# Second norm of a decoder layer in two column halves, two up units opened together, and the group differences spread over the products

## Chip, cores and metric

One core of one Trainium2 chip runs the kernel. The metric is the device time of one execution in microseconds (us), the median of several runs.

## What is computed

One decoder layer over 2048 prompt tokens and 8 x 4 sample tokens, D = 1024, DFF = 2816, all in float32:

```python
h = rms_norm(x, norm1_g) * (1 + scale1) + shift1
...
x = x + gate1 * (jnp.concatenate([o_sb, o_mlp], axis=-1) @ w_out)
h2 = rms_norm(x, norm2_g) * (1 + scale2) + shift2
up = h2 @ w_up
conv = conv_b + sum(conv_w[i] * buf[:, i:i + t] for i in range(CONV_W))
g_ff, v_ff = jnp.split(conv, 2, axis=-1)
x = x + gate2 * ((jax.nn.silu(g_ff) * v_ff) @ w_down)
```

The convolution is causal and three wide; `buf` is `up` with its two predecessor rows in front (the halo). The sample tokens also attend over 8192 cached positions that are read page by page.

## The kernel before

The kernel has four stages; the change lies in the last, `finish_layer`. It holds its activations transposed: 128 features on the partitions, tokens along the free axis. The prompt is worked in four chunks of 512 tokens (c = 0 to 3); the 32 sample tokens ride with chunk 3, so that its tiles are 544 wide.

A chunk is a list of 38 **units** (`unit_order`): 4 out units (w_out), 22 up units (one 128-column pair of gate and value each), and 12 down units in three groups of four (depths 8, 8 and 6 tiles of `hidden`), slipped in between the up units as soon as their part of `hidden` exists. A unit is a 2 x 2 block product done in **seven products** (a Strassen-Winograd scheme) instead of eight: products 1, 2, 6, 5, 7, 3, 4 in that order, each of four matmuls 128x128 by 128x256 (three in the last down group; a matmul leaves two records). Four weight sums (`weight_sums`, GpSimd, L1675 to L1680) belong to each unit, and four **differences** of the moving operand (`difference`, VectorE, L1531) to each group of units that share it: one set for the out units, one for the up units, three for the down groups. Product 6 of a group's first unit needs two of the four, product 7 three, product 4 all.

`product_order` writes the order of the 266 products of a chunk: product 1 of a unit, then product 4 of the unit before, then 2, 6, 5, 7, 3; only the last out unit and the last unit close with their own product 4 straight behind 3. `multiply` (L1368) issues them. Four PSUM banks serve two units in turn; a product that reuses a bank waits until its last result is drained: in up units by ScalarE for products 1, 6, 5, 4 (`collect`, L1461) and by VectorE for 2, 7, 3 (`combine`, L1591); in out and down units by VectorE for all seven (`add_gated`, L1555, which adds into x).

`chunk_plan` interleaves the rest with the products, and every engine walks the same list in order. A product costs 1.75, the steps of the norm are given costs too (3.5, 4, 4, 4, 12, 2: 42.5 in all), and the pieces of the sample attention (SCORE, WEIGH, MOVE, SUM for each of 64 steps, in chunks 0 to 2) are spread evenly over the summed cost. Of a step, SCORE (L962), MOVE (L968) and SUM (L976) are TensorE's, WEIGH (L1051, L1038, L1042) and the copy after MOVE (L1046) VectorE's, the two gates after SCORE (L1011, L1012) ScalarE's. The pages are issued by SyncE in order: K pages of step N when SCORE of N-1 is done, V pages of N when SUM of N-1 is done (L922, L925). Behind the last pages of a chunk SyncE issues the next chunk's input `act_in` (`load_in`, L1300).

**The norm** stands between the last out unit and up unit 0. ScalarE squares x (L1418, L1419), TensorE sums over the partitions with a matrix of ones (L1381; L1383 for the sample columns), ScalarE takes the root (`root`, L1423), VectorE the reciprocal (`invert`, L1627), VectorE and GpSimd multiply four tiles each (`scale`, L1632 and L1694), ScalarE applies gain and shift (`modulate`, L1434), VectorE makes the four up differences. All of it is 512 columns wide.

**The differences** of the down groups stand four in a row behind product 3 of up units 10 and 18; those of the next chunk's out units four in a row behind product 5 of down unit 2 of the last group (chunks 0 and 1) or product 2 of down unit 3 (chunk 2). `first_taps` (VectorE) copies the halo into `raw` (L1605) and the new halo out (L1611), then does two taps of the convolution (L1620; L1622 for the samples); `last_tap` (ScalarE, L1439) does the third ahead of it.

```python
follow = {(AT_UNIT[UP, 10, 0], 3): [("diff", d0, i) for i in range(4)],
          (AT_UNIT[UP, 18, 0], 3): [("diff", d1, i) for i in range(4)],
...
ahead = (AT_UNIT[DOWN, 2, 2], 5) if c < NCH - 2 else (AT_UNIT[DOWN, 3, 2], 2)
```

## Time and profile before

| | us |
|---|---|
| median of 3 runs (3638.83 to 3641.12) | 3639.74 |
| the profiled execution, its own time | 3645.24 |
| span in its profile, first to last instruction | 3643.5 |
| of the span, the last stage from its first product | 1296.9 to 3643.5 |
| chunks 0, 1, 2, 3 of it, each from where the chunk before hands over | 611, 599, 591, 546 |

TensorE's busy time counts a matmul from its start to its modelled end; idle is what lies between. A product starts 1.73 us behind the one before it when nothing holds it. In the timeline, the bracket behind a row gives the idle time ahead of it and what ended it. PEclk, or the granted clock, is the share of 2.4 GHz that TensorE is given: 1 or one half (1.2 GHz).

### The profile page before, as it was taken

How to read it: one execution, taken by the hardware profiler on the slowest of the kernel's cores; microseconds unless marked ns; L12 is line 12 of the kernel's file. 1: busy time of each engine (PE TensorE's matmuls, PEld its weight loads, DVE VectorE, ACT ScalarE, POOL GpSimd, SP SyncE). 2: the span in 40 equal slices, each digit the busy share in tenths (PEclk: the TensorE clock that was granted, in tenths of full speed). 3: DMA queues.
4: the chain of work that ended last, by engine and by line, in shares of the span. 5: the costliest groups of instructions: out<-in, count | busy, mean ns of one | idle time of the engine just before them, and what ended most of it. 6: DMA issues, size and time to landing. Idle time of an engine off the chain costs nothing.

```text
span 3643.5 us, 52814 instructions
## 1 busy us (share of the span) xinstructions
PE 3336.0 (92%) x17743; PEld 2307.4 (63%) x17743; DVE 1717.1 (47%) x2857; ACT 1023.4 (28%) x1958; POOL 1460.7 (40%) x1186
## 2 busy tenths in 40 slices
PE   4799999989989877999988999998899989899999
PEld 1344444446656555777766777777677767687777
DVE  0221212148878625554443563543455455466565
ACT  0221221259888602212101221210221110132110
POOL 0010010136656423545423454543355443465553
PEclk7899999979999988999999999999999999999999
DMA  8411101021010077667678766668776654222222
GB/s 313 165 48 39 55 32 53 23 74 42 8 48 13 15 260 232 226 212 250 204 237 267 233 227 208 208 216 275 242 238 209 217 193 156 77 81 70 72 79 76
DMA packets 237933, 536.84 MB, mean 147 GB/s; under 512 B 26831, under 2 KB 60351, under 8 KB 217705
## 3 DMA queue, kind: packets, MB, share of 16 engines
q1 hardware_dynamic: 207081, 361.36, 30.4%
q10 hardware_dynamic: 30592, 172.24, 13.4%
q8 instruction: 135, 2.21, 0.3%
q14 instruction: 125, 1.02, 0.1%
HBM read 498.96 MB, written 34.55 MB: 146 GB/s over the span
## 4 chain that ended last, share of the span: by engine, by line
PE 50%; DVE 7%; issue 3%; DMA 2%; SPq 2%; ACT 0%; POOL 0%; DVEq 0%; POOLq 0%
PE ff_pB L1368 44%; PE s_pZ L962 3%; PE s_pO L976 3%; DVE ff_diff_down L1531 1%; DVE ff_conv L1620 1%; DMA s_kpage<-in_cache_k 1%; DVE s_left L1038 1%; DMA ff_act_in<-scratch_catT 1%; SPq L914 1%; DVE ff_halo L1611 1%; DVE ff_x L1555 1%; SPq L922 1%; DVE ff_hidden L1531 0%; DVE ff_raw L1605 0%; ACT ff_conv L1439 0%
## 5 line engine op out<-in xcount | busy, mean ns | idle before, releaser
L1368 PE MATMUL ff_pB<-ff_act_in,ff_w 128*128 128x256 f32 (+1 forms) x2496 | 609.6, 388 | 32.7 <-DMA ff_act_in<-scratch_catT 18.2
L1368 PEld LDWEIGHTS ff_pB<-ff_act_in,ff_w 128*128 128x128 f32 x2496 | 470.6, 191 | 138.6 <-issue 53.2
L1675 POOL TENSOR_TENSOR ff_sums<-ff_w 128x512 f32<-128x512 f32 (+1 forms) x152 | 190.2, 1251 | 806.5 <-PE ff_pB L1368 680.1
L417 PE MATMUL in_pA<-in_w,in_hT 128*128 128x512 f32 (+1 forms) x1024 | 450.6, 595 | 1.0 <-DVE in_hT L536 1.0
L1368 PE MATMUL ff_pB<-ff_diff_up,ff_sums 128*128 128x256 f32 (+1 forms) x1664 | 402.4, 385 | 4.1 <-DVE ff_diff_up L1531 4.1
L1555 DVE SCALAR_TENSOR_TENSOR ff_x<-ff_pB,k_mod,ff_x 128x256 f32<-128x256 f32 (+2 forms) x448 | 213.8, 480 | 402.8 <-PE ff_pB L1368 401.2
L856 POOL TENSOR_TENSOR at_stop<-at_stop,at_left 128x512 f32<-128x512 f32 (+3 forms) x320 | 311.1, 997 | 182.4 <-ACT at_stop L796 176.9
L1461 ACT ACTIVATE ff_raw<-ff_pB 128x256 f32<-128x256 f32 (+1 forms) x352 | 136.6, 388 | 822.7 <-PE ff_pB L1368 822.7
L1368 PEld LDWEIGHTS ff_pB<-ff_diff_up,ff_sums 128*128 128x128 f32 x1664 | 313.4, 190 | 67.5 <-issue 16.3
L1591 DVE TENSOR_TENSOR ff_raw<-ff_raw,ff_pB 128x256 f32<-128x256 f32 (+1 forms) x264 | 112.2, 425 | 512.1 <-PE ff_pB L1368 511.6
L417 PEld LDWEIGHTS in_pA<-in_w,in_hT 128*128 128x128 f32 (+1 forms) x1024 | 186.6, 186 | 233.2 <-issue 232.0
L1620 DVE SCALAR_TENSOR_TENSOR ff_conv<-ff_raw,k_vecT,ff_conv 128x512 f32<-128x512 f32 x352 | 318.1, 904 | 6.2
L1368 PE MATMUL ff_pB<-ff_hidden,ff_w 128*128 128x256 f32 (+1 forms) x1056 | 263.0, 391 | 0.6 <-DVE ff_x L1555 0.5
L1368 PE MATMUL ff_pB<-ff_diff_down,ff_sums 128*128 128x256 f32 (+1 forms) x704 | 187.7, 411 | 69.2 <-DVE ff_x L1555 68.8
L1687 POOL TENSOR_TENSOR ff_raw<-ff_raw,ff_conv 128x512 f32<-128x512 f32 (+1 forms) x88 | 114.0, 1295 | 338.4 <-ACT ff_raw L1444 128.5
L844 DVE TENSOR_TENSOR_SCAN at_left<-at_go,at_left,at_one 128x512 f32<-128x512 f32 x192 | 234.8, 1265 | 2.5 <-ACT at_go L796 1.1
L1439 ACT ACTIVATE ff_conv<-ff_raw,k_vecT 128x512 f32<-128x512 f32 (+1 forms) x176 | 144.5, 821 | 307.9 <-DVE ff_raw L1591 304.9
L1680 POOL TENSOR_TENSOR ff_sums<-ff_w,ff_sums 128x512 f32<-128x512 f32 (+1 forms) x152 | 226.0, 1487 | 11.9
L1368 PEld LDWEIGHTS ff_pB<-ff_hidden,ff_w 128*128 128x128 f32 x1056 | 203.7, 195 | 42.6 <-issue 8.3
L1678 POOL TENSOR_TENSOR ff_sums<-ff_w 128x512 f32<-128x512 f32 (+1 forms) x152 | 220.6, 1451 | 11.9
L614 POOL TENSOR_TENSOR in_kn<-in_kraw,k_kg 128x512 f32<-128x512 f32 (+1 forms) x17 | 21.5, 1265 | 464.8 <-DVE in_kraw L558 464.8
L1368 PEld LDWEIGHTS ff_pB<-ff_diff_down,ff_sums 128*128 128x128 f32 x704 | 138.8, 202 | 107.0 <-issue 70.6
(181 smaller groups left out, 4814.9 us busy)
## 6 DMA issues: line engine op xcount, KB each, us to landing
ff_w<-in_w_units ACTq DMA_DIRECT2D x136, 1024.0 KB, 5.9
s_kpage<-in_cache_k SPq DMA_DIRECT2D x512, 256.0 KB, 3.6
s_vpage<-in_cache_v SPq DMA_DIRECT2D x512, 256.0 KB, 3.2
wada<-in_w_ada SPq DMA_DIRECT2D x8, 3072.0 KB, 12.3
ff_w<-in_w_units ACTq DMA_DIRECT2D x16, 768.0 KB, 4.9
in_w<-in_w_in SPq DMA_DIRECT2D x5, 2048.0 KB, 19.6
in_x<-in_x_prompt SPq DMA_DIRECT2D x16, 512.0 KB, 6.1
ff_act_in<-scratch_catT SPq DMA_DIRECT2D x4, 2048.0 KB, 15.4
```

What stands on the lines that cost most here:

```text
L417: last = pe.matmul(pA[0:R, m % 2, :], hT[:, kt, t * R:(t + 1) * R], w[:, kt, col:col + DSB], start=kt == 0, stop=kt == KT - 1)
L844: dve.tensor_tensor_scan(left[:, e, x0:x1][:, ::-1], go[:, r, e, c:KC][:, ::-1], other, first, ALU.mult, ALU.bypass).then_inc(left_ready, 1)
L856: pool.tensor_tensor(w, w, left[:, e, x0 + 1:x1 + 1], ALU.mult).then_inc(w_ready, 1)
L1368: last = pe.matmul(into, left[:, kt * P:(kt + 1) * P], right[:, kt, :], start=kt == 0 and p in (1, 2, 5), stop=kt == depth(j) - 1, skip_gr ...
L1439: act.activation(conv[:, f % 2, half, 0:width(c)], raw[:, f % 2, half, 2:2 + width(c)], ACT.Identity, scale=k["vecT"][:, 196 + ft:197 + ft ...
L1461: act.activation(dst, C if p == 5 else A, ACT.Copy).then_inc(taken, 1)
L1555: dve.scalar_tensor_tensor(x[:, d, lo:hi], bank[:, 0:hi - lo], mod, x[:, d, lo:hi], ALU.mult, ALU.add).then_inc(added, 1)
L1620: ins = dve.scalar_tensor_tensor(cv, raw[:, f % 2, half, i:i + CT], tap, cv, ALU.mult, ALU.add)
L1675: pool.tensor_tensor(S3, A11, A21, ALU.subtract).then_inc(sums_ready, 1)
L1678: pool.tensor_tensor(S2, A21, A11, ALU.subtract).then_inc(sums_ready, 1)
L1680: pool.tensor_tensor(S4, A12, S2, ALU.subtract).then_inc(sums_ready, 1)
L1687: pool.tensor_tensor(sg, sg, conv[:, f % 2, 0, 0:width(c)], ALU.mult).then_inc(silu_ready, 1)
```

## The change

Five things, all in `finish_layer` and its plan:

- The norm is done in two column halves (256 wide, 272 in chunk 3): sums, root, reciprocal, scaling, gain and shift of half 0, then of half 1. The squares of the last out unit's two tiles move from ScalarE to VectorE (`square_last`), in halves, and its product 4 ahead of its product 3. The sums of the first six tiles stand between products 7 and 4. The separate sums of the sample columns go.
- Up units 0 and 1 are opened together: products 1, 1, 2, 2, which need only half 0; then 6, 5, 7, 3, 4 of unit 0, then 6, 5, 7, 3 of unit 1. The taps of unit 0 move with them (`tap_at`).
- The down differences stand one by one behind products of up units 9 and 10 (group 0), 17 and 18 (group 1) and down unit 3 (group 2); those of the next chunk behind products 2 and 7 of down units 2 and 3 (chunks 0 and 1) or 2, 6, 7, 3 of down unit 3 (chunk 2). Group 2 and the out group exchange their buffers of differences.
- The halo copies move from VectorE to ScalarE, behind `last_tap`; those of the sample columns stay.
- The norm's events and the differences cost nothing in the plan, so that the pieces of sample attention stand evenly among products alone.

The diff, cut to its core:

```diff
 def product_order():
 
+
     order = []
     for j in range(NU):
-        order.append((j, 1))
-        if j not in (0, HALVES):
-            order.append((j - 1, 4))
-        order += [(j, p) for p in (2, 6, 5, 7, 3)]
-        if j in (HALVES - 1, NU - 1):
+        if j not in (HALVES, HALVES + 1):
+            order.append((j, 1))
+            if j:
+                order.append((j - 1, 4))
+            order.append((j, 2))
+        elif j == HALVES:
+            order += [(j, 1), (j + 1, 1), (j, 2), (j + 1, 2)]
+        if j == HALVES - 1:
+            order += [(j, p) for p in (6, 5, 7, 4, 3)]
+        else:
+            order += [(j, p) for p in (6, 5, 7, 3)]
+        if j in (HALVES, NU - 1):
             order.append((j, 4))
     return order
 
-              (AT_UNIT[DOWN, 3, 1], 4): [("diff", d2, 3)]}
+    follow = {}
+    for key, places in (((DOWN, 0), (((UP, 9, 0), 5), ((UP, 9, 0), 3), ((UP, 10, 0), 6), ((UP, 10, 0), 7))),
+                        ((DOWN, 1), (((UP, 17, 0), 5), ((UP, 17, 0), 3), ((UP, 18, 0), 6), ((UP, 18, 0), 7))),
+                        ((DOWN, 2), (((DOWN, 3, 1), 6), ((DOWN, 3, 1), 5), ((DOWN, 3, 1), 7), ((DOWN, 3, 1), 3)))):
+        for i, (unit, p) in enumerate(places):
+            follow[AT_UNIT[unit], p] = ("diff", key, i)
     if not last:
-        ahead = (AT_UNIT[DOWN, 2, 2], 5) if c < NCH - 2 else (AT_UNIT[DOWN, 3, 2], 2)
-        follow[ahead] = [("diff", (OUT, 0), i) for i in range(4)]
+        places = ((2, 2), (2, 7), (3, 2), (3, 7)) if c < NCH - 2 else ((3, 2), (3, 6), (3, 7), (3, 3))
+        for i, (q, p) in enumerate(places):
+            follow[AT_UNIT[DOWN, q, 2], p] = ("diff", (OUT, 0), i)
     for j, p in PRODUCTS:
         events.append((("mul", j, p), 1.75 * depth(j) / HALVES))
-        events += [(event, 0.0) for event in follow.get((j, p), ())]
+        if (j, p) in follow:
+            events.append((follow[j, p], 0.0))
         if p == 4 and UNIT[j][0] == OUT and UNIT[j][1] < HALVES - 1:
             events.append((("square", UNIT[j][1]), 0.0))
+        if (j, p) == (HALVES - 1, 7):
+            events += [(("sumsq", q), 0.0) for q in range(HALVES - 1)]
         if (j, p) == (HALVES - 1, 3):
-            events += [(("sumsq", q), 3.5) for q in range(HALVES - 1)]
-        if (j, p) == (HALVES - 1, 4):
-            events += [(("square", HALVES - 1), 4.0), (("sumsq", HALVES - 1), 4.0), (("root",), 4.0), (("scale",), 12.0)]
-            events += [(("diff", (UP, 0), i), 2.0) for i in range(4)]
+            events += [((kind, half), 0.0) for half in range(2) for kind in ("sumsq_end", "root")]
+            events += [(("scale", half), 0.0) for half in range(2)]
+            events += [(("diff", (UP, 0), i), 0.0) for i in range(2)]
+        if (j, p) == (HALVES + 1, 2):
+            events += [(("diff", (UP, 0), i), 0.0) for i in range(2, 4)]
     pieces = [(q, i) for q in steps for i in (SCORE, WEIGH, MOVE, SUM)]
     close = AT_UNIT[DOWN, 2, 1] if NSTEP - 1 in steps else NU
     total = sum(cost for event, cost in events if event[0] != "mul" or event[1] < close)
...
-            T2, T3, T4 = (diff[DOWN if kind == DOWN else UP][:, q, 0:n, 0:H] for q in range(3))
+            T2, T3, T4 = (diff[UP if kind == UP or g == 2 else DOWN][:, q, 0:n, 0:H] for q in range(3))
             return src[:, lo, 0:H], src[:, lo, H:W], src[:, hi, 0:H], src[:, hi, H:W], T2, T3, T4
...
+            H = width(c) // 2
+            return slice(H, CT) if half else slice(0, H)
+
+
+        def tap_at(j, n):
+            return (6, 5, 7)[n] if j == HALVES + 1 else (1, 2, 6)[n]
...
 
-            def sum_squares(c, q):
-
+
+            def sum_squares(c, half, d):
+                H = width(c) // 2
+                return pe.matmul(pB[half][:, 0:H], k["ones"][:], hidden[:, d, half * H:half * H + H], start=d == 0, stop=d == KT - 1)
+
+            def sum_pair(c, q):
                 if q == 0:
                     drained(pe, c, HALVES - 2, 4)
                     drained(pe, c, HALVES - 2, 3)
-                pe.wait_ge(squared, HALVES * c + q + 1)
-                for n, d in enumerate((q, HALVES + q)):
-                    ends = dict(start=q == 0 and n == 0, stop=q == HALVES - 1 and n == 1)
-                    last = pe.matmul(pB[0][:], k["ones"][:], hidden[:, d, 0:CT], **ends)
-                    if c == NCH - 1:
-                        last = pe.matmul(pB[1][:, 0:S], k["ones"][:], hidden[:, d, CT:CW], **ends)
-                if q == HALVES - 1:
-                    last.then_inc(summed, 1)
+                pe.wait_ge(squared, (HALVES - 1) * c + q + 1)
+                for half in range(2):
+                    for d in (q, HALVES + q):
...
-                act.wait_ge(summed, c + 1)
-                ins = act.activation(rs[:, 0:CT], pB[0][:], ACT.Sqrt, scale=1.0 / D, bias=k["eps"][:])
-                if c == NCH - 1:
-                    ins = act.activation(rs[:, CT:CW], pB[1][:, 0:S], ACT.Sqrt, scale=1.0 / D, bias=k["eps"][:])
-                ins.then_inc(rooted, 1)
-
-            def modulate(c):
+            def root(c, half):
+                H = width(c) // 2
+                act.wait_ge(summed, 2 * c + half + 1)
+                act.activation(rs[:, half * H:half * H + H], pB[half][:, 0:H], ACT.Sqrt, scale=1.0 / D, bias=k["eps"][:]).then_inc(rooted, 1)
+
+            def modulate(c, half):
...
+                at = 2 * ups(c, f) + half + 1
+                if at <= 2 * FT:
+                    act.wait_ge(halo_zero, 1)
+                else:
+                    act.wait_ge(halo_out, at - 2 * FT)
+                act.activation(raw[:, f % 2, half, 0:2], halo[:, :, ft], ACT.Copy).then_inc(halo_in, 1)
+                act.wait_ge(halo_in, at)
+                act.activation(halo[:, :, ft], raw[:, f % 2, half, CT:CT + 2], ACT.Copy).then_inc(halo_out, 1)
...
+                    if j == HALVES:
+                        drained(act, c, j, 3)
+                        last_tap(c, f, 0)
                     drained(act, c, j, 4)
                     drained(act, c, j, 7)
                     last_tap(c, f, 1)
-                if p == 6 and earlier is not None:
...
-                elif kind == DOWN and g:
+                    dve.wait_ge(prod_done, prod(c - 1, AT_UNIT[DOWN, HALVES - 1, 1], 4))
+                elif kind == DOWN and g == 0:
+                    dve.wait_ge(prod_done, prod(c, HALVES - 1, 4))
+                elif kind == DOWN and g == 1:
                     if i:
-                        dve.wait_ge(prod_done, prod(c, AT_UNIT[DOWN, HALVES - 1, g - 1], (0, 6, 7, 4)[i]))
-                elif kind == DOWN and c:
-                    dve.wait_ge(prod_done, prod(c - 1, NU - 1, 4))
+                        dve.wait_ge(prod_done, prod(c, AT_UNIT[DOWN, HALVES - 1, 0], (0, 6, 7, 4)[i]))
+                elif kind == DOWN:
+                    dve.wait_ge(prod_done, prod(c, AT_UNIT[UP, FT - 1, 0], 4))
                 into, one, two = ((B12, B12, B11), (T2, B22, B12), (T3, T2, B11), (T4, B21, T2))[i]
                 dve.tensor_tensor(into, one, two, ALU.subtract).then_inc(diffs_ready, 1)
...
+            def square_last(c, p):
+                H, q = width(c) // 2, HALVES - 1
+                parts = {2: ((q, 0),), 4: ((KT - 1, 0),), 3: ((q, 1), (KT - 1, 1))}.get(p, ())
+                for d, half in parts:
+                    drained(dve, c, q, p)
+                    if c == NCH - 1 and half:
+                        dve.wait_ge(gated_s, HALVES)
+                    cols = slice(half * H, half * H + H)
+                    dve.tensor_tensor(hidden[:, d, cols], x[:, d, cols], x[:, d, cols], ALU.mult).then_inc(squared_dve, 1)
 
             def combine(c, j, p):
...
                 ft = half * FT + f
                 at = 2 * ups(c, f) + half + 1
-                into, kept, tail = raw[:, f % 2, half, 0:2], halo[:, :, ft], raw[:, f % 2, half, CT:CT + 2]
                 sample = c == NCH - 1
                 r_s = raw[:, f % 2, half, 2 + CT:2 + CW].rearrange("p (b s) -> p b s", s=TS) if sample else None
                 cv_s = conv[:, f % 2, half, CT:CW].rearrange("p (b s) -> p b s", s=TS) if sample else None
                 near = ring_s[:, f % 2, half, :, :]
 
                 dve.wait_ge(convolved, at)
-                ins = dve.tensor_copy(into, kept)
                 if sample:
                     dve.tensor_copy(near[:, :, 0:2], halo_s[:, ft, :, :])
-                    ins = dve.tensor_copy(near[:, :, 2:6], r_s)
-                ins.then_inc(halo_in, 1)
+                    dve.tensor_copy(near[:, :, 2:6], r_s).then_inc(near_in, 1)
+                    dve.wait_ge(near_in, 2 * f + half + 1)
+                    dve.tensor_copy(halo_s[:, ft, :, :], r_s[:, :, 2:4]).then_inc(halo_s_out, 1)
                 dve.wait_ge(halo_in, at)
-                ins = dve.tensor_copy(kept, tail)
-                if sample:
-                    ins = dve.tensor_copy(halo_s[:, ft, :, :], r_s[:, :, 2:4])
-                ins.then_inc(halo_out, 1)
                 for i in (1, 0):
                     tap = k["vecT"][:, 108 + FT * 2 * i + ft:109 + FT * 2 * i + ft]
                     if i == 0:
...
```

## Rows read from the trace of the kernel before

**Rows 1.** Busy us by stretch, PEclk, DMA: a steady stretch; the four chunks' sum.
```profile
1400.00:1560.00 160.00, 158.60 (x931) 122.28 (x924) 86.25 (x142) 43.77 (x87) 81.20 (x59) 0.99 0.73 239
...
sum 2346.60, PE 2183.43 PEld 1696.30 DVE 1164.22 ACT 438.12 POOL 1076.05; mean PE 545.86 PEld 424.07 DVE 291.05 ACT 109.53 POOL 269.01
```

**Rows 2.** Waits of TensorE in the last stage: us in total, times, longest.
```profile
PE ff_pB L1368 <- DVE ff_x L1555: 89.5, 28, 10.2
PE s_pZ L968 <- DVE s_stop L1042: 23.0, 5, 9.5
PE s_pZ L962 <- DMA s_kpage<-in_cache_k: 17.7, 6, 5.0
PE s_pO L976 <- DVE s_wT L1046: 7.4, 3, 6.3
```

**Rows 3.** Timeline of TensorE around the norm of chunk 0: start, us, what, idle before.
```profile
1377.69 2.74 PE L962 MATMUL s_pZ<-s_kpage,s_q 128*32 128x256 f32 x32 [3.28 <-DMA s_kpage<-in_cache_k]
1389.98 0.69 PE L968 MATMUL s_pZ<-k_ident,s_stop 128*128 128x128 f32 x2 [9.55 <-DVE s_stop L1042]
1397.00 3.64 PE L976 MATMUL s_pO<-s_vpage,s_wT 128*32 128x512 f32 x16 [6.33 <-DVE s_wT L1046]
```

**Rows 4.** Timeline of VectorE in the same norm.
```profile
1383.35 3.35 DVE L1627 RECIPROCAL ff_rs<-ff_rs 128x512 f32<-128x512 f32 x1 [12.18 <-ACT ff_rs L1423]
1389.85 6.76 DVE L1632 TENSOR_TENSOR ff_act_in<-ff_x,ff_rs 128x512 f32<-128x512 f32 x4
```

**Rows 5.** Timeline of ScalarE and GpSimd in the norm of chunk 1.
```profile
1987.17 1.28 ACT L1423 ACT_TABLE_LOAD   x1
1989.25 0.69 ACT L1423 ACTIVATE ff_rs<-ff_pB,k_eps 128x512 f32<-128x512 f32 x1 [0.80 <-PE ff_pB L1381]
1993.41 6.81 POOL L1694 TENSOR_TENSOR ff_act_in<-ff_x,ff_rs 128x512 f32<-128x512 f32 x4 [26.14 <-DVE ff_rs L1627]
```

**Rows 6.** Timeline of TensorE around the norm of chunk 3.
```profile
3161.78 1.12 PE L1381 MATMUL ff_pB<-ff_hidden,k_ones 128*128 128x512 f32 x2 [2.22 <-ACT ff_hidden L1419]
3173.34 5.96 PE L1368 MATMUL ff_pB<-ff_act_in,ff_w 128*128 128x272 f32 x16 [9.20 <-ACT ff_act_in L1434]
3183.41 3.13 PE L1368 MATMUL ff_pB<-ff_diff_up,ff_sums 128*128 128x272 f32 x8 [4.12 <-DVE ff_diff_up L1531]
```

**Rows 7.** Timeline at the first group difference of chunk 0, VectorE and TensorE.
```profile
1569.86 2.28 DVE L1531 TENSOR_TENSOR ff_diff_down<-ff_hidden,ff_diff_down 128x1024 f32<-128x1024 f32 x1
1574.40 3.75 PE L1368 MATMUL ff_pB<-ff_diff_down,ff_sums 128*128 128x256 f32 x8 [5.99 <-DVE ff_x L1555]
1577.95 2.94 PE L1368 MATMUL ff_pB<-ff_hidden,ff_w 128*128 128x256 f32 x8
...
1584.50 1.89 PE L1368 MATMUL ff_pB<-ff_hidden,ff_sums 128*128 128x256 f32 x8
1586.23 1.89 PE L1368 MATMUL ff_pB<-ff_act_in,ff_w 128*128 128x256 f32 x8
```

**Rows 8.** Timeline where chunks 0, 1 and 2 hand over to the next.
```profile
1888.17 0.43 SPq L1300 DMA_DIRECT2D ff_act_in<-scratch_catT  x1
1902.82 1.23 DVE L1531 TENSOR_TENSOR ff_act_in<-ff_act_in 128x1024 f32<-128x1024 f32 x1 [8.49 <-DMA ff_act_in<-scratch_catT]
1908.14 1.22 PE L1368 MATMUL ff_pB<-ff_diff_down,ff_w 128*128 128x256 f32 x2 [10.24 <-DVE ff_x L1555]
...
2507.02 2.93 PE L1368 MATMUL ff_pB<-ff_diff_down,ff_w 128*128 128x256 f32 x6 [9.20 <-DVE ff_x L1555]
...
3097.46 1.56 PE L1368 MATMUL ff_pB<-ff_diff_down,ff_sums 128*128 128x256 f32 x6 [3.44 <-DVE ff_x L1555]
```

**Rows 9.** A gap behind a down unit in chunk 3, and VectorE's halo copies by form.
```profile
3366.17 2.07 PE L1368 MATMUL ff_pB<-ff_diff_down,ff_sums 128*128 128x272 f32 x8 [1.93 <-DVE ff_x L1555]
...
L1611 DVE COPY ff_halo<-ff_raw 128x2 f32<-128x2 f32 x176 | 96.5, 548 | 6.0
```

**Rows 10.** DMA issues of the page: KB each, median us to landing.
```profile
s_kpage<-in_cache_k SPq DMA_DIRECT2D x512, 256.0 KB, 3.6
```

More of the change, by code:

```diff
@@ L1465, in collect @@
                     last_tap(c, f, 1)
-                if p == 6 and earlier is not None:
+                if p == tap_at(j, 2) and earlier is not None:
                     gate(c, earlier)
@@ L1582, in combine @@
                 earlier = UNIT[j - 1][1] if j and UNIT[j - 1][0] == UP else None
-                if p == 1 and earlier is not None:
+                if p == tap_at(j, 0) and earlier is not None:
                     first_taps(c, earlier, 0)
```

95 lines of the change are left out of this document (53 added, 42 removed).

## The prediction

> **What bounds the kernel now.** I read the busy time by stretch first. In a steady stretch of up units TensorE is busy 158.6 of 160 us at a granted clock of 0.99, while VectorE has 86 and GpSimd 81 [rows 1]: products stand back to back, and nothing on another engine shortens them. Over the four chunks it is busy 2183 of 2347 us, so 163 us are idle [rows 1]. Hence only idle time, and the slow products behind it, can be saved. The list of waits says where it lies: 89.5 us in 28 waits on VectorE's adds into x, and 23.0, 17.7 and 7.4 us on pieces of the sample attention [rows 2]. The adds are only last in a queue: the timeline shows what stood ahead of them. I sort the gaps by place; each place shows one pattern.
>
> - *Norms* (four). Chunk 0: 3.28 + 9.55 + 6.33 us [rows 3]; chunk 3: 2.22 + 9.20 + 4.12 us [rows 6]. Chunks 1 and 2 hold the rest of the three attention waits: 23.0 + 17.7 + 7.4, less chunk 0's 19.2, the 5.0 us wait for pages at the stage's start (the longest of its row) and 0.6 in small ones, is 23.3. Sum: 19.2 + 15.5 + 23.3 = 58.0 us.
> - *Down differences of groups 0 and 1* (eight). Four differences in a row, 2.13 to 2.28 us each, hold VectorE for 8.7 us; the product behind waits 5.99 us [rows 7]. The eight are between 2.3 and 6.7 us, 44.3 in all. (Group 2 leaves no gap.)
> - *Hand-over to the next chunk* (three): 10.24, 9.20 and 3.44 us [rows 8], 22.9 in all. In the first two VectorE sits in its first difference until the next input has landed: issued at 1888.17, used at 1902.82, 14.65 us later [rows 8].
> - *Others*: 19 us, four of about 2.3 us in chunks 0 to 2 and five of 1.93 in chunk 3, where taps and halo copies stand ahead of an add [rows 9].
>
> **Slow products.** Behind a long gap TensorE runs at the lower of its two clocks (1.2 GHz) for some microseconds. Behind the 5.99 us gap two products take 3.75 and 2.94 us, where one at 2.4 GHz takes 1.89 and starts 1.73 us behind the last [rows 7]. From start to start that costs 3.55 - 1.73 and 2.87 - 1.83, 2.8 us. Added up in this way: 13 us in the norms, 18 at the differences, 4 at hand-overs, 3 elsewhere. A gap and its slow products cost about 1.4 times the gap.
>
> **The change part by part.**
>
> *Down differences one by one.* Each of the 32 follows a product alone. Such a product leaves VectorE an add of some 0.4 us in 1.73; a difference of 2.28 us makes it late by one product, and what it is late for (the drain of product 7, wanted by product 4) is three products off. In an up unit of about 13 us VectorE has half its time free (86 of 160 [rows 1]), room for two differences of 4.5. So nearly all 44.3 + 18 = 62 us go. What is late next: a WEIGH piece ahead of an add. In chunk 0 WEIGH 9 falls behind product 1 of the first down unit and its MOVE two products later, right behind the last difference; I leave 2 to 3 us for it, and 4 in all. **-58**, bounds -63 and -40 (half of each gap back at four places).
>
> *The norm in halves.* Let T be the end of product 3 of the last out unit. Its product 4 is already added; the sums of six tiles (four 256-wide matmuls a pair, as many columns as before) cover it. Then in chunks 1 and 2:
>   1. Sums of half 0 end at T+0.9, root at T+1.4 (0.69 us for 512 columns [rows 5], some 0.45 for 256). The table load of 1.28 us starts ahead of the last sums (1987.17, root at 1989.25 [rows 5]), so it is hidden behind product 3.
>   2. VectorE adds product 3, squares twice, a WEIGH piece ahead: free at T+2.1. Sums of half 1 end at T+3.0.
>   3. Reciprocal of half 0: 3.35 / 2 = 1.7 [rows 4], T+3.8. VectorE and GpSimd multiply by turns: 6.76 us for four tiles each at 512 [rows 4], 3.4 at 256. Half 0 is done at T+7.2, its first four tiles, with gain and shift, at about T+5.9.
>   4. TensorE: product 1 of up units 0 and 1 from T+5.9, both 2's, done at about T+13. Idle so far 0.8 + 2.9.
>   5. Half 1: reciprocal to T+8.7, multiplications to T+12, two differences of 1.2 to 2.3 each to T+15.5. Product 6 opens there: 2.5 us idle.
> So 6 us idle in each of chunks 1 and 2. In chunk 0 SUM 2 stands behind the first product 2 and needs VectorE's copy from behind the two differences, which puts SUM and one product (3.6 us) behind the wait: 8.5. Chunk 3 has three small operations for the sample columns between: 8.3. Together 29 against 58, and slow products 9 against 13; the sample columns' sums save 1. **-34**. Bounds: -48 (differences at 1.2, waits of 3 us a chunk) and -15 (the halves cost as much as the whole, next paragraph).
>
> Turns of VectorE and GpSimd are the step that could fail. The trace has 6.76 and 6.81 us for 4 + 4 tiles [rows 4, 5]; a linear half is 3.4. The Trainium skill ("SBUF — State Buffer", "Who interferes with whom") says that the pair of ports these two engines share is an exclusive lock held for a whole instruction. That the two spans agree to 0.05 us fits it. By that rule the fixed cost of each instruction is serial too and halves don't halve: some 0.3 us a pair, 2.4 a chunk, and the sum would end about 5 to 10 us higher.
>
> *The hand-over gets worse.* Pieces now stand 4.93 apart in cost, not 5.39 (chunk 0: 453.25 / 92 and 495.75 / 92). SUM of the last step but one, which frees SyncE to issue the last V pages and then the input, comes two products later (2.6 us). The first difference now follows product 2, not 5, so VectorE blocks three products earlier. Before: TensorE resumed four differences and an add behind the landing (1902.82 to 1908.14 = 5.3 [rows 8]). After: one difference and an add, 1.9, then the three products that used to be ahead of the stall, 3.9, of which some are slow. 2.6 + 1.9 + 3.9 - 5.3 + 1.4 is about 4.5 us per hand-over in chunks 0 and 1. In chunk 2 the input is there long before; single differences of 1.3 fit between products of 1.3 with little wait: -2.5. **+6.5**, bounds 0 and +15.
>
> *Halo copies to ScalarE.* They took 0.55 us a piece on average on VectorE [rows 9], most of that waiting. ScalarE gets two of about 0.2 us behind each of 176 taps; its result of product 1 is wanted 3.5 us later, so this is covered. The five gaps of 1.93 us lose their larger part (-6), those of 2.3 us a third (-3, slow products included). **-9**, bounds -19 and +5.
>
> *Opening two units together, the exchanged buffers, product 4 before 3*: nothing. The weights of up unit 1 were issued 30 us before; its weight sums are needed eight products later than its product 1.
>
> **The sum**: -58 - 34 + 6.5 - 9 = -94.5. From the profiled execution's 3645.2 that is 3550.7; the median stands 5.5 below it (3639.7), so 3545.
>
> **The rivals.**
>
> *The norm gives nothing back* (0.14). Halves cost fixed time twice, and the differences wait for GpSimd in each: then -15 or less. For it: the port turns; against: product 1 no longer waits for all eight tiles. 3639.7 - 58 - 15 + 6.5 - 9, about 3565.
>
> *Single differences leave waits behind* (0.12): at eight places 2 us and 1.5 of slow products, 28 us. For it: the 2.3 us gaps where a single WEIGH does this. About 3573.
>
> *The hand-over grows further* (0.08): landing 5 us later in denser traffic and slow products: +15 instead of +6.5. About 3554, or 3560 with slower page loads elsewhere.
>
> *Nearly every gap goes* (0.09): port waits vanish where steps are short: all three bounds, about 3515.
>
> *Slower than before* (0.03): the page supply becomes the bound. The place: SCORE of a step waits for its K pages, which SyncE issues only behind the V pages, 1 us each. A step takes about 23.4 us of TensorE instead of 25.1. V issue (8 to 9 us), K issue (8) and landing 3.6 us [rows 10] need some 21 of the 28 from SUM to the next SCORE but one. DMA is at 0.73 and 239 GB/s [rows 1] and would be at 0.78. It decides when pages land more than 10 us behind their issue: then each of 64 steps waits, and at over 1.6 us each the saving is gone; at 2 us, 3639.7 - 94.5 + 128 = 3673. Against: in steady stretches no page is waited for; the waits are where pieces crowd, in the norms.
>
> **How the numbers follow.** My forecast has 0.54; its own range, from the bounds taken half way, is 3525 to 3570. The rivals above it reach to 3573, the one below to 3515. With the ends of the bounds (-63 - 48 + 0 - 19 = -130; -40 - 15 + 15 + 0 = -40) the range is 3510 to 3598; outside lie the slower rival and stacked bounds. A measurement here can tell 0.2%, 7 us, from no change. Every case but the last is faster by more: faster 0.95, same 0.01, slower 0.04 (with a little for a stall that I don't see).
>
> **What would show it.** Right: no gap over 1 us before the first products 6 and 7 of down groups 0 and 1; differences standing alone at 1.2 to 2.3 us; four products (1, 1, 2, 2) behind the norm's sums, with one gap of about 3 us ahead and one of 2 to 4 behind; hand-over gaps of 12 to 14 us in chunks 0 and 1 in front of a product 7, none of note in chunk 2; no wait for K pages but the first. Wrong: norm idle of over 12 us a chunk, multiplications of half a width taking over 4.5 us for four; new waits on ScalarE's results in up units; waits for pages in steady stretches.

## The result, and the profile after

The changed kernel took 3550.97 us (median of 4, 3546.94 to 3552.62) against 3640.43 for the kernel before (4 runs, 3638.83 to 3641.41): a ratio of 0.9753, interval 0.9736 to 0.9770, so 2.5% faster. The forecast was 3545.0 with 3510 to 3598. Profiled execution against profiled execution it is 3550.62 against 3645.24, 94.6 us less, where the forecast's sum was 94.5; by the medians it is 89.5.

TensorE's waits in the last stage (us in total, times, longest) answer to [rows 2]:

```profile
PE ff_pB L1391 <- DVE ff_x L1600: 48.1, 22, 12.4
PE ff_pB L1391 <- DMA ff_act_in<-scratch_catT: 18.0, 1, 18.0
PE ff_pB L1391 <- ACT ff_act_in L1466: 13.4, 4, 3.5
PE s_pZ L968 <- DVE s_stop L1042: 5.7, 8, 1.9
PE s_pZ L962 <- DMA s_kpage<-in_cache_k: 4.9, 1, 4.9
```

The adds into x fell from 89.5 to 48.1 us, and the three attention waits from 48.1 to 12.8 with the third, 2.2 us, which is not shown. Of the adds' 48.1, the two longest are the hand-overs (12.4 and 12.3). K pages are waited for once, at the stage's start, as forecast.

Counted by place, TensorE's idle time in the last stage (its start included) fell from 178.2 to 107.7 us. Its products at the lower clock cost 23.1 us, not 43.2 (half of TensorE's busy time in the stretches whose granted clock was 0.5). Together that is 90.6 of the 94.6 us; the rest is that the stage began 4.4 us earlier in this execution. The places are:

| idle us | before | after | forecast |
|---|---|---|---|
| four norms | 58.0 | 23.7 | 29 |
| down differences, groups 0 and 1 | 44.3 | 9.1 | 4 |
| hand-overs | 22.9 | 26.2 | some 27 |
| others of 1.8 us and more | 19.1 | 16.1 | 12 |

The norm of chunk 1, by the timeline (start, us, what, idle before), answers to [rows 4, 5]:

```profile
1948.67 1.89 PE L1391 MATMUL ff_pB<-ff_act_in,ff_sums 128*128 128x256 f32 x8
...
1949.23 1.28 ACT L1456 ACT_TABLE_LOAD   x1 [10.05 <-PE ff_pB L1391]
...
1951.46 0.47 ACT L1456 ACTIVATE ff_rs<-ff_pB,k_eps 128x256 f32<-128x256 f32 x1 [0.94 <-PE ff_pB L1399]
1951.56 0.76 DVE L1630 TENSOR_TENSOR ff_hidden<-ff_x 128x256 f32<-128x256 f32 x2
1952.23 1.75 DVE L1682 RECIPROCAL ff_rs<-ff_rs 128x256 f32<-128x256 f32 x1
...
1954.01 3.02 DVE L1689 TENSOR_TENSOR ff_act_in<-ff_x,ff_rs 128x256 f32<-128x256 f32 x4
1954.06 3.56 POOL L1749 TENSOR_TENSOR ff_act_in<-ff_x,ff_rs 128x256 f32<-128x256 f32 x4 [21.26 <-DVE ff_rs L1682]
...
1956.78 5.38 PE L1391 MATMUL ff_pB<-ff_act_in,ff_w 128*128 128x256 f32 x16 [3.28 <-ACT ff_act_in L1466]
...
1962.22 3.62 PE L1391 MATMUL ff_pB<-ff_act_in,ff_w 128*128 128x256 f32 x16
...
1963.36 1.31 DVE L1576 TENSOR_TENSOR ff_act_in<-ff_act_in 128x1024 f32<-128x1024 f32 x1 [1.59 <-ACT ff_act_in L1466]
...
1966.93 1.99 PE L1391 MATMUL ff_pB<-ff_diff_up,ff_sums 128*128 128x256 f32 x8 [1.09 <-DVE ff_diff_up L1576]
```

Product 3, the first row, ended at T = 1950.56. The root was done at T+1.4 (forecast 1.4), the first half was multiplied at T+7.1 (7.2), product 1 began at T+6.2 (5.9), product 6 at T+16.4 (15.5). Four products stand between, two of them slow (5.38 us for both), which is why only 1.09 us of idle time are left in front of product 6. Half a width costs half: 3.56 us for four tiles on GpSimd, where the whole took 6.81 [rows 5].

The first group's differences in chunk 0 answer to [rows 7]. Here are three of the four, and TensorE's rows just behind the last:

```profile
1523.30 1.22 DVE L1576 TENSOR_TENSOR ff_diff_down<-ff_hidden 128x1024 f32<-128x1024 f32 x1
...
1531.98 1.22 DVE L1576 TENSOR_TENSOR ff_diff_down<-ff_diff_down,ff_hidden 128x1024 f32<-128x1024 f32 x1
...
1537.78 1.22 DVE L1576 TENSOR_TENSOR ff_diff_down<-ff_hidden,ff_diff_down 128x1024 f32<-128x1024 f32 x1
...
1546.19 0.44 PE L968 MATMUL s_pZ<-k_ident,s_stop 128*128 128x128 f32 x2 [1.88 <-DVE s_stop L1042]
1546.46 1.89 PE L1391 MATMUL ff_pB<-ff_diff_down,ff_sums 128*128 128x256 f32 x8
```

The gap of 5.99 us is gone, and the MOVE behind WEIGH 9 waits 1.88 us where the forecast had put it. These three take 1.22 us each, where four in a row took 2.13 to 2.28 (the first, at 1520.02, still has 2.29: GpSimd was in a gate multiplication, L1742, that had begun at 1519.89).

The hand-over of chunk 0 answers to [rows 8]:

```profile
1842.88 8.40 SPq L925 DMA_DIRECT2D s_vpage<-in_cache_v  x8
...
1851.32 0.43 SPq L1322 DMA_DIRECT2D ff_act_in<-scratch_catT  x1
...
1866.01 1.23 DVE L1576 TENSOR_TENSOR ff_act_in<-ff_act_in 128x1024 f32<-128x1024 f32 x1 [12.79 <-DMA ff_act_in<-scratch_catT]
...
1867.69 2.93 PE L1391 MATMUL ff_pB<-ff_diff_up,ff_sums 128*128 128x256 f32 x6 [12.39 <-DVE ff_x L1600]
```

SyncE issues eight V pages first, then the input; VectorE sits 12.79 us in its first difference, and TensorE waits 12.39 us for the add queued behind it.

### The profile page after: what moved, and what is told of

It is laid out like the page before. It is cut to its first block, busy times and chain, and to the rows that moved or that the text cites. A ratio compares the mean times of both kernels' runs of the same rounds, so it can differ in the third digit from the quotient of the medians.

```text
span 3548.9 us, 53129 instructions
## 1 busy us (share of the span) xinstructions
PE 3316.0 (93%) x17790; PEld 2305.7 (65%) x17791; DVE 1679.3 (47%) x2542; ACT 1079.3 (30%) x2337; POOL 1466.9 (41%) x1202
## 4 chain that ended last, share of the span: by engine, by line
PE 54%; DVE 6%; issue 1%; DMA 1%; ACT 1%; SPq 0%; DVEq 0%; ACTq 0%
PE ff_pB L1391 46%; PE s_pZ L962 3%; PE s_pO L976 3%; DVE ff_conv L1673 1%; DMA ff_act_in<-scratch_catT 1%; DVE s_left L1038 1%; PE ff_pB L1399 1%; DVE ff_act_in L1689 0%; DVE ff_x L1600 0%; PE s_pZ L968 0%; DVE s_stop L1042 0%; ACT ff_conv L1471 0%; DVE ff_conv L1675 0%; DVE ff_rs L1682 0%; DVE s_kpage L1666 0%
## 5 line engine op out<-in xcount | busy, mean ns | idle before, releaser
L1728 POOL TENSOR_TENSOR ff_sums<-ff_w 128x512 f32<-128x512 f32 (+1 forms) x152 | 191.1, 1257 | 777.5 <-PE ff_pB L1391 636.4
L1673 DVE SCALAR_TENSOR_TENSOR ff_conv<-ff_raw,k_vecT,ff_conv 128x512 f32<-128x512 f32 x352 | 379.9, 1080 | 84.4 <-ACT ff_raw L1478 78.2
L1391 PE MATMUL ff_pB<-ff_diff_up,ff_sums 128*128 128x256 f32 (+1 forms) x1600 | 391.0, 387 | 29.3 <-DVE ff_x L1600 24.7
L1391 PEld LDWEIGHTS ff_pB<-ff_diff_up,ff_sums 128*128 128x128 f32 x1600 | 301.8, 191 | 94.7 <-DVE ff_x L1600 25.5
L1733 POOL TENSOR_TENSOR ff_sums<-ff_w,ff_sums 128x512 f32<-128x512 f32 (+1 forms) x152 | 220.1, 1448 | 11.9
L1731 POOL TENSOR_TENSOR ff_sums<-ff_w 128x512 f32<-128x512 f32 (+1 forms) x152 | 211.9, 1394 | 11.9
L1729 POOL TENSOR_TENSOR ff_w<-ff_w 128x512 f32<-128x512 f32 (+1 forms) x152 | 207.5, 1365 | 0.0
```

The lines of the kernel that those rows point to most:

```text
L1391: last = pe.matmul(into, left[:, kt * P:(kt + 1) * P], right[:, kt, :], start=kt == 0 and p in (1, 2, 5), stop=kt == depth(j) - 1, skip_gr ...
L1673: ins = dve.scalar_tensor_tensor(cv, raw[:, f % 2, half, i:i + CT], tap, cv, ALU.mult, ALU.add)
L1728: pool.tensor_tensor(S3, A11, A21, ALU.subtract).then_inc(sums_ready, 1)
L1729: pool.tensor_tensor(A21, A21, A22, ALU.add).then_inc(sums_ready, 1)
L1731: pool.tensor_tensor(S2, A21, A11, ALU.subtract).then_inc(sums_ready, 1)
L1733: pool.tensor_tensor(S4, A12, S2, ALU.subtract).then_inc(sums_ready, 1)
```

## The experiments

Each was timed in five rounds beside the kernel before. "Us" below is the ratio to it, times 3640; the change itself is -90 (interval ±6). Ratios have intervals of ±0.1 to 0.2%, so a difference between two kernels is uncertain by some 6 to 9 us. Where an expectation names theories A and B, A or B below says which one the run bears out.

**Four differences in a row again** (groups 0 and 1), all else as changed:

```diff
-    for key, places in (((DOWN, 0), (((UP, 9, 0), 5), ...)),
-                        ((DOWN, 1), (((UP, 17, 0), 5), ...)),
-                        ((DOWN, 2), ...)):
+    rows4 = {(AT_UNIT[UP, 10, 0], 3): (DOWN, 0), (AT_UNIT[UP, 18, 0], 3): (DOWN, 1)}
+    for key, places in (((DOWN, 2), ...),):
...
+        if (j, p) in rows4:
+            events += [(("diff", rows4[j, p], i), 0.0) for i in range(4)]
```

> The changed kernel (3551.0 us), in which only the down differences of groups 0 and 1 stand again four in a row behind product 3 of up units 10 and 18. Theory A (each difference alone fits between two products; this part was worth what the gaps before show): the eight gaps come back, 44.3 us idle with 18 us of slow products, less the 6.8 us idle and 3.4 us slow that the single ones still leave: about +52 us, 3603 us. Theory B (much of the gain at these places came from elsewhere, the halo copies that left VectorE and the new places of the attention pieces): four in a row leave gaps of 3 us or less, under +30 us, below 3581 us. The trace decides by the gaps ahead of products 2 or 6 of the first down unit: 5 to 6 us under A, 3 or less under B.

Measured: 0.9856 (0.9837 to 0.9875), -52: putting them back costs 38 us. The eight gaps are 35.9 us, not 44.3: 7.15, 6.58 and 6.59, three of 3.9, and two of about 2. Between A and B; the next two runs say why.

**The kernel before with single differences alone** (the diff's plan lines for the three groups, buffers and waits):

> The kernel before (3640.4 us) with this part of the change alone: down differences of all three groups one by one, with the buffers exchanged; norm, halo copies and product order as before. Theory A (the parts add up): -48 to -56 us, 3584 to 3592 us, norms still 58 us idle. Theory B (the parts lean on each other, single differences fit only because the halo copies are gone from VectorE): the gaps fall by half only, -30 us, 3610 us.

Measured: 0.9885 (0.9865 to 0.9904), -42: between A and B, nearer to A. At the down differences 13.8 us of idle time are left in gaps over 1 us, where the changed kernel has 9.1; chunk 3 has two gaps of 2.90 and two of 1.08 us there. So the single differences fit without the other parts, but not as well.

**The kernel before with the halo copies alone on ScalarE**:

```diff
 def last_tap(c, f, half):
+                act.activation(raw[:, f % 2, half, 0:2], halo[:, :, ft], ACT.Copy).then_inc(halo_in, 1)
+                act.wait_ge(halo_in, at)
+                act.activation(halo[:, :, ft], raw[:, f % 2, half, CT:CT + 2], ACT.Copy).then_inc(halo_out, 1)
 def first_taps(c, f, half):
-                ins = dve.tensor_copy(into, kept)
...
-                ins = dve.tensor_copy(kept, tail)
```

> The kernel before (3640 us) with the halo copies of the taps on ScalarE and nothing else changed (those of the sample columns stay on VectorE). Theory A (the prediction's term): -9 us, 3631 us. Theory B (the copies were part of what stood in VectorE's queue at the down differences too, whose gaps add up to 35.9 us, not 44.3, where four stand in a row without the copies): the down gaps shrink to about 36 us, most in groups 1 of chunks 0 and 2, and with the small waits in the up units it is -18 to -22 us, 3618 to 3622 us.

Measured: 0.9974 (0.9965 to 0.9984), -9.5: A. The down gaps sum to 42.5 us here, so B is wrong: the copies took hardly 2 us of them. What then made them 35.9 in the first experiment is what TensorE had to do meanwhile. The second group of chunk 0, in this kernel and in the first experiment's (timelines of TensorE):

```profile
1745.67 1.24 PE L1370 MATMUL ff_pB<-ff_hidden,ff_w 128*128 128x256 f32 x5
1752.84 3.75 PE L1370 MATMUL ff_pB<-ff_diff_down,ff_sums 128*128 128x256 f32 x8 [5.93 <-DVE ff_x L1565]
```

```profile
1726.85 1.92 PE L976 MATMUL s_pO<-s_vpage,s_wT 128*32 128x512 f32 x16
1728.71 1.99 PE L1392 MATMUL ff_pB<-ff_diff_up,ff_w 128*128 128x256 f32 x8
1730.54 1.89 PE L1392 MATMUL ff_pB<-ff_hidden,ff_w 128*128 128x256 f32 x8
1736.32 3.75 PE L1392 MATMUL ff_pB<-ff_diff_down,ff_sums 128*128 128x256 f32 x8 [3.90 <-DVE ff_x L1601]
```

In the new plan, with the norm's piece costs at zero, a SUM piece of 1.92 us falls into the stall and covers that much of it: 5.93 becomes 3.90. It can go the other way too: the first group of chunk 0 has 7.15 us in the first experiment and 5.71 here. So the price of a row of four depends on the plan around it.

**The halo copies back on VectorE**, all else as changed:

> The changed kernel with the two halo copies of each tap back on VectorE (those of the sample columns stayed there anyway). By the prediction's term this costs 9 us (3560 us). By what the trace after shows (three gaps of about 2.3 us in chunks 0 to 2 and five of 1.9 us in chunk 3 are still there with the copies gone) it costs nothing that can be measured: 3548 to 3555 us. A third way: the single differences need the time that the copies left, and gaps open ahead of the adds in the up units that hold two differences: 10 us or more.

Measured: 0.9797 (0.9780 to 0.9814), 16 us slower than the changed kernel: the third way. VectorE's copies and taps of chunks 0 to 2 in this kernel, and the taps in the changed one (busy us, mean ns, idle before):

```profile
L1667 DVE SCALAR_TENSOR_TENSOR ff_conv<-ff_raw,k_vecT,ff_conv 128x512 f32<-128x512 f32 x264 | 268.3, 1016 | 4.6
...
L1661 DVE COPY ff_halo<-ff_raw 128x2 f32<-128x2 f32 x132 | 62.7, 475 | 4.5
...
L1654 DVE COPY ff_raw<-ff_halo 128x2 f32<-128x2 f32 x132 | 42.6, 323 | 69.1 <-ACT ff_conv L1471 69.1
```

```profile
L1673 DVE SCALAR_TENSOR_TENSOR ff_conv<-ff_raw,k_vecT,ff_conv 128x512 f32<-128x512 f32 x264 | 309.9, 1175 | 82.9 <-ACT ff_raw L1478 78.2
```

The copies hold VectorE for 105 us; without them the taps themselves wait longer (1175 ns, not 1016), which takes back 42. The rest is real, and much of it is small waits. Of the 11.2 us more idle time in the stage, 6.5 are gaps of 0.2 to 1 us (31 of them, 17.1 us in all, against 19 with 10.6), and the down differences leave 13.3 us, not 9.1.

**The norm of before**, all else as changed (built from the kernel before with single differences, the next input's too, buffers and halo copies):

> The changed kernel with the norm, the product order and the piece costs of the kernel before: only the single differences (all groups, the next input's too), the exchanged buffers and the halo copies on ScalarE are kept. Theory A (the parts stand for themselves): the norms go from 24 us idle back to 58, slow products from 9.4 us to 13, and the sample columns' own sums come back: +37 to +39 us, 3588 to 3590 us. Theory B (part of the norm's gain came from the other parts): +25 us or less, 3576 us.

Measured: 0.9834 (0.9820 to 0.9847), -60: the norm (with its place in the plan) is worth 30 us, between the two. Its idle time comes back to 52 us rather than 58 (chunk 0's norm has two gaps here, the third is covered), and the hand-overs shrink from 12.4 and 12.3 us to 10.1 and 10.0, probably since the old piece costs bring SUM earlier: a gain that the norm's share has to pay.

**Up units 0 and 1 not opened together**:

```diff
-        elif j == HALVES:
-            order += [(j, 1), (j + 1, 1), (j, 2), (j + 1, 2)]
+        order.append((j, 1))
+        if j not in (0, HALVES):
+            order.append((j - 1, 4))
+        order.append((j, 2))
```

> The changed kernel with up units 0 and 1 no longer opened together: behind the norm only products 1 and 2 of up unit 0, then 6, which needs two differences. Theory A: the pair covers the second half of the norm. In chunk 1 product 6 was reached with only 1.09 us idle after four products; with two it comes two products earlier, so about 3.5 us more idle in each chunk and about 1 us more of slow products: +15 to +20 us, 3566 to 3571 us. Theory B: the halves alone do it, the second half's chain being hidden behind products 1 and 2: +5 us or less.

Measured: 0.9792 (0.9774 to 0.9810), 14 us slower: A. In chunk 1 (TensorE):

```profile
1961.27 5.38 PE L1388 MATMUL ff_pB<-ff_act_in,ff_w 128*128 128x256 f32 x16 [3.28 <-ACT ff_act_in L1463]
1971.40 3.45 PE L1388 MATMUL ff_pB<-ff_diff_up,ff_sums 128*128 128x256 f32 x8 [4.53 <-DVE ff_diff_up L1570]
```

4.53 us ahead of product 6 instead of 1.09, and product 6 itself is slow. In the four norms the idle time is 35.6 us, not 23.7. About half of the norm's 30 us is the pair. The other half is the rest of the new norm, two column halves and the squares on VectorE among it, which was not taken apart further. The pair also has a cost that the forecast put at nothing. The changed kernel has one new gap in chunk 3, in front of an up product shortly behind the norm:

```profile
3128.58 2.10 PE L1391 MATMUL ff_pB<-ff_act_in,ff_w 128*128 128x272 f32 x8 [2.28 <-DVE ff_raw L1649]
```

It isn't there without the pair, nor with the norm of before, nor where the sample columns' copies are on ScalarE.

**The next input issued before the last V pages**:

```diff
                     for of_keys in (True, False):
+                        if c < NCH - 2 and N == STEPS[c][-1] and not of_keys:
+                            load_in(c + 1)
...
-                load_in(c + 1)
+                if c == NCH - 2:
+                    load_in(c + 1)
```

> The changed kernel in which SyncE issues the next chunk's input (2 MB into act_in) ahead of the last V pages of chunks 0 and 1, not behind them; in chunk 0 that is at about 1836 us of the trace, not 1851, and the last reader of the old input is done by then. Theory A (the hand-over waits for nothing but this landing, 14.7 us after the issue): both gaps of 12.3 to 12.4 us go, with their slow products (9.05 us at half clock, so about 4.5 us lost): -25 to -29 us, 3522 to 3526 us. Theory B (the input now shares the DMA queues with the last V pages and the next K pages, which come late): gaps in front of SUM or SCORE pieces at the chunk's end take the place of half or more, 3537 us or more.

Measured: 0.9676 (0.9661 to 0.9690), 3523.93 us, 28 less than the changed kernel: A. SyncE and VectorE at the hand-over of chunk 0:

```profile
1840.32 0.45 SPq L1322 DMA_DIRECT2D ff_act_in<-scratch_catT  x1
...
1847.62 8.71 SPq L925 DMA_DIRECT2D s_vpage<-in_cache_v  x8
...
1857.89 1.22 DVE L1579 TENSOR_TENSOR ff_act_in<-ff_act_in 128x1024 f32<-128x1024 f32 x1
```

The difference starts with no wait in front of it. No gap over 1 us is left at either hand-over, nor has another wait taken its place.

**The next input's differences back in a row, later**:

> The changed kernel with the differences of the next chunk's input back in a row where they stood: behind product 5 of the third last down unit (chunks 0 and 1), behind product 2 of the last in chunk 2. Theory A (the early place makes the gap longer, as the prediction has it): the two gaps begin three products later and end three differences later: from 12.4 to about 10 or 11 us each, and about 2 us more idle in chunk 2; net 0 to -3 us. Theory B (only the landing counts, and four in a row behind it cost more than the place): +3 to +8 us.

Measured: 0.9758 (0.9743 to 0.9772), 2 us slower, no difference that can be told. The gaps were 11.9, 9.1 and 3.4 us, 1.7 us less in all than with them single, while slow products cost 28.0 us in the stage, not 23.1. The runs can't tell A from B here; the place of these differences is worth nothing that can be told.

**All eight multiplications on VectorE**:

```diff
-                for kt in range(0, KT, 2):
+                for kt in range(KT):
                     dve.tensor_tensor(act_in[:, kt, cols], x[:, kt, cols], rs[:, cols], ALU.mult).then_inc(scaled_dve, 1)
...
-                    if j == HALVES:
-                        scale(c)
```

> The changed kernel with all eight multiplications of each half of the norm on VectorE, none on GpSimd. Theory A (VectorE and GpSimd take turns, so that the second engine adds nothing): a 256-column multiplication alone takes about 0.33 to 0.4 us, eight of them 2.7 to 3.2 us, where VectorE's four took 3.02 and GpSimd's four 3.56: the same or 0.5 us shorter for each half, 3545 to 3552 us. Theory B (the two engines really share the work): eight take twice VectorE's 3.02, some 6 us, and each norm grows by 3 to 6 us idle: +20 us or more, 3571 us.

Measured: 0.9761 (0.9748 to 0.9775), 3 us slower, not told from no change. The timeline of chunk 1 shows both what was tested and what hid it:

```profile
1953.38 1.54 POOL L1724 TENSOR_TENSOR ff_sums<-ff_w 128x512 f32<-128x512 f32 x1 [17.90 <-PE ff_pB L1391]
...
1954.22 2.38 DVE L1626 TENSOR_TENSOR ff_hidden<-ff_x 128x256 f32<-128x256 f32 x2
...
1963.39 2.77 DVE L1685 TENSOR_TENSOR ff_act_in<-ff_x,ff_rs 128x256 f32<-128x256 f32 x8
```

Eight tiles on VectorE alone take 2.77 us; four there beside four on GpSimd took 3.02 and 3.56. For these multiplications the second engine was worth less than nothing: A. The Trainium skill ("Perfetto Trace Analysis", "Optimizing Scalar/DVE Operations") says that moving work between these two might not help, since they share a port; here it costs 0.8 us a half. But GpSimd, now free, begins the next weight sums, and the last two squares take 2.38 us beside them, not 0.76.

**The sample columns' small copies on ScalarE** (chunk 3):

> The changed kernel with the three small copies of the sample columns (chunk 3 alone, 1.2 to 1.3 us the ones that wait) on ScalarE too, behind the halo copies. Theory A (VectorE's queue is too long by these copies): the five gaps of 1.85 us in chunk 3 go, and the two of 2.4 us shrink: -8 to -12 us, 3539 to 3543 us. Theory B (what VectorE waits for is GpSimd's instruction, and the next small instruction on VectorE waits as long): the gaps stay, 0 to -3 us.

Measured: 0.9736 (0.9722 to 0.9750), -6 against the changed kernel, inside its uncertainty and between A and B. By the trace the five gaps of 1.85 us stay, as B has it, but as 1.44; the two of 2.4 us become 2.07 and 2.06, and the one of 2.28 us behind the pair goes. That is 5 us of idle time.

**GpSimd's weight sums three products later**:

```diff
                 if j >= 2:
-                    pool.wait_ge(prod_done, prod(c, j - 2, 3))
+                    pool.wait_ge(prod_done, prod(c, *((j - 2, 3) if j == HALVES + 2 else (j - 1, 2))))
```

> The changed kernel with GpSimd's four weight sums of each unit started behind product 2 of the unit before, not behind product 3 of the one before that, three products or some 5 us later (not at the pair). Theory A (the gaps of 1.85 and 2.3 us are VectorE's small instructions, each ending with one of GpSimd's): the sums no longer meet the first taps, those gaps go, -8 to -15 us, 3536 to 3543 us. Theory B (the sums then meet the second taps and the adds, and hold up the gated products behind them): the gaps move, new ones open ahead of products 6 and 7, 0 to +15 us.

Measured: 0.9817 (0.9804 to 0.9831), 23 us slower: B in kind, and more than its 15 us. A gap of 1.85 us is one of 3.38 now (chunk 3, the three engines):

```profile
3312.68 1.28 POOL L1729 TENSOR_TENSOR ff_w<-ff_w 128x512 f32<-128x512 f32 x1
3312.87 1.12 DVE L1666 COPY s_kpage<-ff_raw 128x16 f32<-128x16 f32 x1
...
3314.05 1.73 POOL L1731 TENSOR_TENSOR ff_sums<-ff_w 128x512 f32<-128x512 f32 x1
3314.57 1.25 DVE L1675 SCALAR_TENSOR_TENSOR ff_conv<-s_kpage,k_vecT,ff_conv 128x32 f32<-128x32 f32 x1
...
3318.35 3.76 PE L1391 MATMUL ff_pB<-ff_diff_down,ff_sums 128*128 128x272 f32 x8 [3.38 <-DVE ff_x L1600]
```

A copy of 16 columns takes 1.12 us, one of the same kind 0.17 where GpSimd is idle (at 3307.49 in this trace): VectorE's small operations end just behind the end of a GpSimd operation (3312.68 + 1.28 = 3313.96 and 3312.87 + 1.12 = 3313.99). The sums must run somewhere, and behind product 2 they meet the second taps, with the adds behind them.

**Three together**: the early input, the sample copies, and the multiplications on VectorE with GpSimd held back until two differences are made:

```diff
                     if j == HALVES:
-                        scale(c)
+                        pool.wait_ge(diffs_ready, diffs_made(c, UP, 0, 2))
```

> The changed kernel with three things: the next input issued ahead of the last V pages, the sample copies on ScalarE, and all eight multiplications of the norm on VectorE while GpSimd's next weight sums are held back until two differences are made (without that hold they ran beside the squares, which took 2.38 us for two, not 0.76). Theory A: -27 for the input, -5 for the copies, and in each norm 0.3 us less ahead of product 1 and about 1 us less ahead of product 6, since two differences take 1.2 us each with GpSimd still: -4 to -6 in all; 3512 to 3516 us. Theory B (the held sums are late for product 6 of up unit 1, or meet the other two differences): the norm part is 0 or a loss, 3518 us or more.

Measured: 3506.27 us (3503.57 to 3515.86), 0.9636 (0.9621 to 0.9651): 3.6% faster than the kernel before and 43 us faster than the changed one, with the same computation. A, and some 6 us more than it said. Norm of chunk 1:

```profile
1936.80 0.76 DVE L1638 TENSOR_TENSOR ff_hidden<-ff_x 128x256 f32<-128x256 f32 x2
...
1943.73 2.77 DVE L1694 TENSOR_TENSOR ff_act_in<-ff_x,ff_rs 128x256 f32<-128x256 f32 x8
...
1949.52 1.22 DVE L1584 TENSOR_TENSOR ff_diff_up<-ff_act_in 128x1024 f32<-128x1024 f32 x1
...
1950.80 1.99 PE L1394 MATMUL ff_pB<-ff_diff_up,ff_sums 128*128 128x256 f32 x8
```

The squares are short again, the second difference takes 1.22 us, and product 6 is no longer waited for. Together with the two other parts (-28 and -6) this leaves about 8 us for the norm, where 4 to 6 were expected, the same within what the runs can tell. The four norms' idle time is 17.8 us, not 23.7.

## Why the prediction was right, step by step

Taken in one order, the parts are measured against each other: the kernel before, with the halo copies -9.5, with the single differences too (the next input's among them) -60.4, with the norm and its plan too -89.9. Each step is uncertain by some 4 to 8 us:

| part | forecast | measured in this order |
|---|---|---|
| halo copies | -9 | -9.5 |
| differences one by one | -58 | -51 |
| norm, pair and hand-over | -34 + 6.5 = -27.5 | -29.5 |

*Differences one by one*: right in kind, 7 us too large, about what the runs can tell. Left over are 9.1 us of gaps, not 4. The WEIGH that the forecast named in chunk 0 is there (1.88 us); it missed two such waits of 1.14 us in chunks 1 and 2, and chunk 3, where two gaps of 2.46 and 2.44 us stay, each with slow products behind it:

```profile
3247.16 3.76 PE L1391 MATMUL ff_pB<-ff_diff_down,ff_sums 128*128 128x272 f32 x8 [2.46 <-DVE ff_x L1600]
```

That is the first product 6 of a down group. The prediction had named no gap over 1 us there as a sign of being right, so this sign holds in chunks 0 to 2 and fails in chunk 3. VectorE's queue holds the sample copies there, which take 0.94 and 1.12 us beside GpSimd's weight sums. Nor is the gain a fixed number: in the kernel before single differences bring 42 us, in the changed one taking them away costs 38. The forecast added up gaps as if each belonged to one cause. A stall of VectorE is shortened by any piece that TensorE has to do in it, and with a new plan a SUM had come to lie there.

*The norm*: each step came within 0.9 us, and the idle time is 23.7 us against 29. Chunk 0 had 6.1 us, not 8.5; the others 5.3, 4.5 and 7.8 (forecast 6, 6 and 8.3). The gap behind the pair is less in chunks 1 and 2 than the 2 to 4 us forecast (1.09 and 0.24), in part since the two products 1, at half the clock, filled the time. The step that was called the one which could fail held: halves do halve. The second column half is hidden as described, and the pair that hides it is worth 14 us of the 30. The rule quoted there from the Trainium skill ("SBUF — State Buffer", "Who interferes with whom"), that the two engines' shared ports are locked for a whole instruction, agrees with what the experiments showed, eight tiles alone being faster than four beside four. What was drawn from it was wrong: a fixed cost that would spoil the halves is not seen (3.56 against 6.81 / 2 = 3.4 us).

*The hand-over*: 12.39 and 12.31 us in front of a product 7, and 1.51 in chunk 2, as forecast (12 to 14, and none of note). The gaps grew by 2.2 and 3.1 us. The run with the norm of before has the old piece costs and the new places, and gaps of 10.1 and 10.0: so some 2.3 us of each come from the later SUM (forecast 2.6), and next to nothing from the places (forecast 1.9 + 3.9 - 5.3 = 0.5), which the time of the run with the old places bears out. This split rests on single traces: in the other runs that keep the new places and the new plan the same two gaps lie between 10.2 and 12.6 us. In chunk 2 the gap shrank by 1.9 us (forecast 2.5, slow products included). All three together grew by 3.3 us, and their slow products by under 1, so the term of +6.5 was too large by 2 to 3 us. That the landing is the cause of the whole stall was shown: with it earlier, both gaps go.

*Halo copies*: the sum was right and the reason wrong. The forecast took 6 us from the five gaps of 1.93 us and 3 from those of 2.3. They are 1.85 and 2.26 now, all five of the first and two of the four second. With the copies alone moved all nine are there (1.85 and 1.86, and 2.09 to 2.27 us). In chunk 3 the sample copies come next in the queue and take the same wait for GpSimd. With the copies alone moved, the stage's idle time is 168.9 us instead of 178.2. Of these 9.3 us, 3.7 are gaps under 1 us, 1.9 the down differences, and the rest lies in small parts in other places. The 0.55 us "a piece" was that of one of the two copies (L1611); the other (L1605) took 0.36. The term did not use it. The same window as in [rows 1], in that kernel, has TensorE busy 159.50 us of 160, not 158.60:

```profile
sum 160.00, PE 159.50 PEld 124.75 DVE 80.59 ACT 49.82 POOL 85.99; mean PE 159.50 PEld 124.75 DVE 80.59 ACT 49.82 POOL 85.99
```

With single differences in the queue the copies matter more: 16 to 19 us. The forecast had no such interaction; at 9 us it is as large as the uncertainty of the runs that it is worked out from, so its size stays open.

*Pairing at no cost and pages in time*: right but for the gap of 2.28 us that the pair brings in chunk 3, a wait for VectorE. No wait for ScalarE's results appeared in the up units, and a K page took 3.9 us to land instead of 3.6 [rows 10].

*The range*: its upper end is added up with 0 for the halo copies, though their bound was +5; with that it is about 3605. Nothing measured depends on it.

The total by the medians is 4.6 us smaller than the sum: 7 lost at the differences, 2.5 gained elsewhere, all of it within what the runs can tell. That the two profiled executions differ by just what was forecast is luck: in the later one the last stage began 4.4 us earlier (its first idle time at 1274.2, not 1278.6), with the stages ahead of it unchanged.

## What to carry to other kernels

Price a stall by what is queued behind it and by what the waiting engine has to do meanwhile; its price changes with the plan, so such terms don't simply add. When a transfer is what an otherwise well hidden hand-over waits for, look at what its queue issues ahead of it: moving one issue past eight others was worth 28 us, as much as the whole new norm. Two engines that take turns were no faster here than one of them for short operations: give such work to the faster one, and keep the other still until the critical part is over.

## What was not expected of the hardware

- VectorE with a GpSimd neighbour: a copy of 16 columns takes 0.17 us, and 1.12 us beside weight sums. Of the changed kernel's 48 differences of 128x1024, the 25 that began while GpSimd stood still took 1.21 to 1.23 us each, and the 23 that began inside a GpSimd operation 1.3 to 2.3, 15 of them 2.12 or more. Before, 29 of the 48 were of the second kind; the four in a row of [rows 7] had weight sums beside them, and spreading them shortened them too. It matters who is first: at 1523.30 a difference took its 1.22 us, and the weight sum that GpSimd began at 1523.78 took 1.87 instead of 1.27.
- Eight multiplications of 128x256 on VectorE take 2.77 us, four on it beside four on GpSimd 3.02 and 3.56.
- Moving copies off VectorE returned 63 of 105 us of its time in chunks 0 to 2: the taps behind them became longer, as if they took over the wait for GpSimd. That reading was not tested by itself.
